# Attention output turned by VectorE in 32x32 blocks straight out of PSUM, put in order by the loads of the next stage, with the join, the expert start and the end re-cut

## The reference

```python
h = rmsnorm(x, g_mix);  z = h @ w_in
o_a = dilated_attention(rope(q_a), rope(k_a), v_a)   # 8 heads of 64
o_b = spatial_gating(uv_b);  o_c = memory_attention(q_c, mem)
o = concat(rmsnorm(o_a), rmsnorm(o_b), rmsnorm(o_c)) * g_out
x = x + o @ w_out
x = x + expert_choice(rmsnorm(x, g_ffn))             # 16 experts, 2*t/16 tokens each
return rmsnorm(x, g_final)
```

## Time and profile before

| | us |
|---|---|
| median of 3 runs | 3288.11 (3286.56 to 3292.55) |
| the profiled execution's own time | 3286.66 |
| its span, first to last instruction | 3284.8 |
| TensorE busy | 3155.9 (96%) |
| VectorE, ScalarE, POOL busy | 1691.6, 1401.4, 731.0 |

### The profile page before, as it was taken

One profiled execution on the slowest core, in us unless ns is written; L12 is line 12 of the kernel. 1 busy time (PEld: TensorE's weight loads), 2 busy tenths in 40 slices (PEclk: granted clock), 3 DMA queues, 4 the chain that ended last, 5 costly groups with the idle time before them and its releaser, 6 DMA issues. The chain is left out here.

```text
span 3284.8 us, 52154 instructions
## 1 busy us (share of the span) xinstructions
PE 3155.9 (96%) x19180; PEld 2749.9 (84%) x19180; DVE 1691.6 (51%) x3631; ACT 1401.4 (43%) x2948; POOL 731.0 (22%) x750
## 2 busy tenths in 40 slices
PE   7999999998999997999689999999999999999996
PEld 5888888886777776888489999999999999999996
DVE  5455545544677775555554444344444344443554
ACT  4333333333788883333343333333333333333443
POOL 0111111113212442222122102222112222112332
PEclk9999999998999998999789999999999999999998
DMA  6222222124744544555347666677666777666895
GB/s 214 61 54 51 55 59 55 47 60 145 242 118 117 161 112 145 189 191 192 118 144 168 142 154 166 165 168 167 136 159 165 168 168 156 144 162 166 230 291 197
DMA packets 389120, 476.13 MB, mean 145 GB/s; under 512 B 131904, under 2 KB 268864, under 8 KB 388800
## 3 DMA queue, kind: packets, MB, share of 16 engines
q1 hardware_dynamic: 368192, 404.35, 45.9%
q0 software_dynamic: 20736, 69.22, 8.4%
HBM read 361.44 MB, written 112.00 MB: 144 GB/s over the span
## 5 line engine op out<-in xcount | busy, mean ns | idle before, releaser
L2115 DVE TENSOR_TENSOR exp_lo<-exp_stage,exp_hi 128x2048 fp32r<-128x2048 f32 x192 | 440.1, 2293 | 566.7 <-ACT exp_hi L1689 566.7
L1689 ACT ACTIVATE exp_hi<-exp_stage 128x2048 fp32r<-128x2048 f32 x192 | 366.6, 1910 | 9.4 <-PE exp_ps_t L2395 4.3
L2380 PE MATMUL exp_ps_g<-exp_xT_hi,exp_lo 128*128 128x384 f32 x1024 | 342.6, 335 | 2.1 <-DVE exp_lo L2115 2.1
L2380 PE MATMUL exp_ps_g<-exp_xT_hi,exp_hi 128*128 128x384 f32 x1024 | 342.3, 334 | 0.0
L2380 PE MATMUL exp_ps_u<-exp_xT_hi,exp_lo 128*128 128x384 f32 x1024 | 342.3, 334 | 0.0
L2380 PE MATMUL exp_ps_g<-exp_xT_lo,exp_hi 128*128 128x384 f32 x1024 | 342.2, 334 | 0.0
L2380 PE MATMUL exp_ps_u<-exp_xT_hi,exp_hi 128*128 128x384 f32 x1024 | 342.1, 334 | 0.0
L2380 PE MATMUL exp_ps_u<-exp_xT_lo,exp_hi 128*128 128x384 f32 x1024 | 342.1, 334 | 0.0
L1926 POOL DMA_INDIRECT scratch_y<-exp_area,route_slots x45 | 91.0, 2023 | 956.4 <-issue 902.0
L1170 ACT ACTIVATE att_prob<-att_prob,att_o 128x256 f32<-128x256 f32 (+1 forms) x576 | 265.8, 464 | 79.2 <-DVE att_o L1212 76.0
L1882 POOL DMA_INDIRECT exp_xe<-scratch_xn,exp_rows_of x180 | 214.8, 1193 | 86.2 <-issue 54.5
(11 more groups left out here) (332 smaller groups left out, 7219.6 us busy)
## 6 DMA issues: line engine op xcount, KB each, us to landing
exp_stage<-in_w_gate SPq DMA_DIRECT2D x256, 256.0 KB, 5.3
exp_stage<-in_w_up SPq DMA_DIRECT2D x256, 256.0 KB, 5.3
exp_stage<-in_w_down SPq DMA_DIRECT2D x256, 256.0 KB, 3.9
out_qT<-scratch_o SPq DMA_DIRECT2D x72, 264.0 KB, 3.0
first_v<-scratch_v SPq DMA_DIRECT2D x64, 256.0 KB, 4.0
scratch_xn<-mix_xn SPq DMA_DIRECT2D x24, 544.0 KB, 3.1
memory_x<-in_x SPq DMA_DIRECT2D x24, 512.0 KB, 3.4
first_v<-scratch_v SPq DMA_DIRECT2D x192, 64.0 KB, 2.2
```

Source lines behind the costliest of these rows:

```text
L1689: self.nc.scalar.activation(self.hi[:, m % self.RW, :, :], self.stage[:, m % self.RS, :, :], ACT.Copy).then_inc(self.hi_sb, 1)
L2115: nc.vector.tensor_tensor(w_lo[:, m % RW, :, :], stage[:, m % RS, :, :], w_hi[:, m % RW, :, :].bitcast(F32), ALU.subtract).then_inc(s["w_l ...
L2380: x_ = nc.tensor.matmul(ps[:, f, 0:S], a[:, m % RW, k, f * P:(f + 1) * P], b[:, k, :], start=(n == 0), stop=(n == 3 * KC - 1))
```

## The change

- `back`, `out_oT` and their buffer go. `out_o` becomes one VectorE transpose in 32x32 blocks, from PSUM to SBUF, waiting for the product itself. Such a transpose moves a block's 32 features onto 32 partitions as queries, and leaves the block's place on the partition axis; so the output's partition axis holds (feature quarter, query), and its columns hold (query quarter, ...). Queries are gathered in a matching order (every fourth one together), the masks, the rows of `w_out` and `g_out` are put into that order ahead of the launch.
- The stores write 512 columns of features and 16 columns of maxima and sums apart, the latter to a new array `stats`: two DMAs a block, and eight for dilation 16 of the sample. For these eight blocks POOL's gather is four copies instead of one.
- The loads of a mixing tile put features in order: 11 DMAs instead of 4. The two that replace `o1` and `o2` are four each (128 pieces of 512 bytes), that of `o0` has 512 pieces.
- The joins of tiles 0 and 1 are spread over the last units of attention (class `Join`), and SP's wait for the last stores moves into mixing, behind its first loads. In every join the last small product is two instructions instead of one, and `scaled3` counts each scaled part.
- Expert start: 8 counting steps ahead of the first product and two in each of units 0 to 3; the turns go tile by tile as each gather lands; the first product waits for five rounds.
- End: the last down product goes tile by tile, and add, square, factor, scale and scatter run as a pipeline over the three tiles. A few semaphores change phase, so that one clearing at the end of the program goes.

```diff
-                    if n % 2 and n > 1:
-                        back(n // 2 - 1)
...
-                    if n % 2 == 0 and n:
-                        out_oT(n // 2 - 1)
...
                 def out_o(c):
-                    dve.wait_ge(back_ps, c + 1)
-                    nc.vector.tensor_copy(o[:, c % RO, 0:D_A], ps_o[:, c % 2, :]).then_inc(o_sb, 1)
+                    dve.wait_ge(pv_ps, 4 * (c + 1))
+                    nc.vector.transpose(o[:, c % RO, 0:D_A], ps_o[:, c % 2, :].rearrange("p (j b i) -> p b j i", j=4, b=QUADS)).then_inc(o_sb, 1)
...
     def load_o(self, sp, A, t, u, seq=0):
...
+        sp.dma_start(to[0], near).then_inc(self.o_loaded[u], 16)
...
+        for a in range(QUADS):
+            sp.dma_start(to[1][:, a, :], mid[a, bass.ds(at * 32, 32)]).then_inc(self.o_loaded[u], 16)
+            sp.dma_start(to[2][:, a, :], far[a, bass.ds(at * 8, 8)]).then_inc(self.o_loaded[u], 16)
+        sp.dma_start(self.o3[:, u, :, D_A:], A["stats"][bass.ds(t * P, P), :, :]).then_inc(self.o_loaded[u], 16)
...
+        T0, T1 = NU - 20, NU - 13
...
+                    for t, at in enumerate((T0, T1)):
+                        if n == at:
+                            join.shift(dve, t, t, 1)
+                        if n == at + 1:
+                            join.divide(dve, t, t)
+                        if at + 2 <= n <= at + 4:
+                            join.scale(dve, t, t, n - at - 2)
+                        if n == at + 6:
+                            join.mean(dve, t)
...
-    FIRST_STEPS = 12
+    FIRST_STEPS = 8
...
+                if m == M - 1 and not more:
+                    for q in range(ST):
...
+                        x_.then_inc(s["tile_done"], 1)
...
+                for q in range(ST):
+                    dve.wait_ge(s["tile_done"], q + 1)
+                    add_end(q, 1)
+                    if q == 0:
+                        mean_end(0)
+                    if q:
+                        scale_end(q - 1)
+                        mean_end(q)
+                scale_end(ST - 1)
```

More of the change, by code:

```diff
@@ L958, in attend_phase @@
+def attend_phase(nc, A, w, early, join, first):
     PIECES = first.PIECES
@@ L1023, in store @@
                     sp.wait_ge(o_sb, c + 1)
-                    for dst, src in blocks[c].outputs(A[f"o{blocks[c].which}"], o[:, c % RO, :]):
+                    for dst, src in blocks[c].outputs(A, o[:, c % RO, :]):
                         sp.dma_start(dst, src).then_inc(o_stored[c % RO], 16)
@@ L1087, in _ @@
                         (lo_w if n % 2 else hi_w)(n // 2)
+                    if c == NB - 4:
+                        nc.gpsimd.memset(join.half[:], -0.5).then_inc(join.s["half_set"], 1)
+                        join.add(pool, 0, 0)
+                    if c == NB - 2:
+                        pool.wait_ge(join.s["half_set"], 1)
+                        join.root(pool, 0)
+                join.add(pool, 1, 1)
+                join.root(pool, 1)
                 pool.wait_ge(w_lo_set, KC)
@@ L1260, in mix_phase @@
         xnT = ph.sb("xnT", [P, KC, P])
[L1261 to L1266, removed]
+        junk, stat, half = join.junk, join.stat, join.half
         ss_y, ms_y, rs_y = stat[:, 100:101], stat[:, 101:102], stat[:, 102:103]
@@ L1350, in fold_lanes @@
                     nc.gpsimd.tensor_tensor(fold[:], fold[:], lane[3], ALU.add).then_inc(s["fold_set"], 1)
[L1352 to L1357, removed]
-                    ge(pool, s["cT_ps"], t - 1)
-                    nc.gpsimd.tensor_tensor(oa[:, u, :], a, c, ALU.add).then_inc(s["added_b"], 1)
-                    pool.wait_ge(s["ms_a"], t + 1)
-                    nc.gpsimd.tensor_tensor(rs_a, ms_a, half[:], ALU.pow).then_inc(s["rs_a"], 1)
                 def norm(t):
@@ L1373, in body @@
                         if not last:
[L1374 to L1376 removed]
+                            join.add(pool, t + 2, u)
+                            join.root(pool, t + 2)
                 fold_lanes()
@@ L1530, in body @@
                         if not last:
-                            join(t + 2, u, i + 2)
+                            join.shift(dve, t + 2, u, i + 2)
+                            join.divide(dve, t + 2, u)
+                            for j in range(3):
+                                join.scale(dve, t + 2, u, j)
                         add_x(t, u, 0, i + 1)
@@ L1864, in _ @@
                 sp.dma_start(g_fin[:], A["g_final"]).then_inc(s["g_loaded"], 16)
-                sp.wait_ge(gathered[0], 16 * ST)
+                for j in range(ST):
+                    sp.wait_ge(first_gathered[j], 16)
                 loop(sp, body)
@@ L1886, in gate @@
                 def gate(e):
-                    pool.wait_ge(gathered[e % 2], gathers(e))
+                    if e:
+                        pool.wait_ge(gathered[e % 2], gathers(e))
+                    else:
+                        for j in range(ST):
+                            pool.wait_ge(first_gathered[j], 16)
                     for a in range(QUADS):
```

380 lines of the change are left out of this document (224 added, 156 removed).

## The result

The changed kernel takes 3343.02 us (median of 4, 3341.63 to 3353.30), against 3288.32 before: ratio 1.0175, 95% interval 1.0155 to 1.0195. It is slower by 55 us where 39 less were forecast. The profiled execution has a span of 3340.3 us.

What follows compares the result with a forecast made beforehand. TensorE bounds attention with dilation 1 and 4 and mixing; a VectorE and ScalarE ring bounds dilation 16. Terms sum to 38.7 us off the profiled 3286.66, 3248.0, so 3249 after allowing for the median; 8 in 10 range 3235 to 3274.

Steps and rivals of the forecast that it cites:

- Attention, TensorE: Dilation 1 and 4 blocks: removing four transposes of `back` saves 0.45 us in each of 48 blocks, 18.0 us after deductions.
- Attention, dilation 16: Dilation 16 blocks: `out_oT` leaves the ring, the transpose takes 0.72 us; 0.43 us a block gained, 10.3 us in all.
- The bound of 1.4 us: Dilation 16: upper bound for the transpose out of PSUM; as a rival (15%), it adds 17 us, giving 3266.
- Attention, costs: Attention: 24 early DMAs instead of 10 lose 2 us (0 to 6); joins of two tiles lose 3 us (0 to 10).
- The hand-over: End of attention to mixing's first product: 9.85 us gained less 1.5 us of SP backlog, 8.3 us (4 to 12).
- The mixing loop: Mixing tiles: SP's 11 loads at 0.43 us, 5.2 us, land before the join needs them; hidden, cost 0.
- the rival on the other side: Mixing: SP's loads become the bound above 1.18 us each; at 1.4 us, 58 us lost, 3307; chance 5%.
- Expert start: Start of experts: first product 0.6 us earlier, four later counting steps cost 1.2; net 0.6 us slower (-1 to +2).
- End: After the last expert product: pipeline over three tiles takes 5.4 us instead of 11.4, 6.0 us gained (4.5 to 7).
- The 0.4 us for the clearing: End of the program: dropping one semaphore clearing gains 0.4 us.

Runs made afterwards that it cites:

- the cut loads of the experiment above: Kernel before, with a tile's dilation 4 and 16 loads cut into four each and dilation 1 into two, 11 DMAs instead of 4, same bytes: 3295.0 us, ratio 1.0026.

## Why the prediction was wrong, step by step

**Attention, TensorE: right for a block.** 6.23 us a block with dilation 1 and 4, 0.44 less. The 18.0 us were too many: the prompt's first 32 blocks brought 11.2, and the sample's first 16, with the early loads spread, 3.4.

**Attention, dilation 16: right for a block, and more.** 4.00 us instead of the 4.14 forecast, and 706 ns for the transpose where 0.72 us was taken. The bound of 1.4 us was not needed.

**Attention, costs: a term mis-sized.** The 24 DMAs were put at 6 us more of SP and 2 us lost; they took 15.6 us of SP where ten took 5, and cost 8. The joins were put at 3 us (0 to 10) and cost about 1. In the changed kernel a VectorE product over 24 columns (L1037) took 2.12 us once, from 1181.27 to 1183.39, while a POOL operation over 1024 columns (L1202) ran from 1180.99 to 1183.36; its median is 0.18. These runs put the whole cost of the joins, such stretching included, at about 1 us.

**The hand-over: a term mis-sized.** Eight stores were priced at 3.6 us and SP's backlog at 1.5 us. Four of the feature stores took 2.7 us and four of the statistics 2.56, so 5.3 a block with the gaps, 6.5 with the values. SP fell behind through all eight blocks and owed 11.8 us at the end. With two stores a block the hand-over was 6.9 us, even better than forecast.

**The mixing loop: the step that failed.** Of the 94 us between the forecast and the result, 64.6 stand here, 19 in attention and 7 in the hand-over. The prediction said "SP's 11 loads at 0.43 ... land near 1415 ... Hidden, 0", and the rival on the other side said that SP decides "once a load costs more than (14 - 1.05) / 11 = 1.18 us". Two things were wrong in that. The price was 0.76 us, not 0.43: the median of 381 ns was that of plain rows, and loads that step through residues were in no row. And the threshold was that of a full queue. SP was never full; the store of `xn` behind the loads closed a ring with VectorE, the turn and the next loads, and in this ring every microsecond past the slack counts at once. The slack can be read from the trace before, had I followed what stands behind the loads on SP. In the tile of the earlier trace rows:

```profile
1408.14 0.33 SPq L945 DMA_DIRECT2D out_qT<-scratch_obc  x1
...
1410.06 0.36 SPq L1308 DMA_DIRECT2D scratch_xn<-mix_xn  x1
...
1415.15 1.28 DVE L1505 SCALAR_TENSOR_TENSOR mix_xn<-out_qT,mix_stat,mix_g_ffn 128x1024 f32<-128x1024 f32 x1 [0.82 <-POOL mix_stat L1366]
```

The store went out 1.6 us after the last load, landed some 3.2 us later (the median) and so was down about 1.9 us before VectorE wrote the buffer again; before the change VectorE never waited for it. That is a slack of some 3.5 us of SP. With 8.4 us of loads from 1406.64 the store could not go before 1415. By this estimate a tile grows by the time of its loads, less the 1.8 us they took before, less 3.5: 0 to 0.2 us for the cut loads of the experiment above (5.3 to 5.5 us; measured 0.3), 3.1 for the 8.4 (measured 3.2 to 4.6 in most tiles, with the slower products in it). The changed kernel has a case between. At the seam of prompt and sample the loads of two tiles stand outside the loop, with no register instructions between them, and take 6.8 us:

```profile
1465.27 0.41 SPq L970 DMA_DIRECT2D out_qT<-scratch_o  x1
...
1471.42 0.60 SPq L977 DMA_DIRECT2D out_qT<-scratch_obc  x1
1472.07 0.43 SPq L1444 DMA_DIRECT2D scratch_xn<-mix_xn  x1
...
1480.59 0.39 SPq L970 DMA_DIRECT2D out_qT<-scratch_o  x1
```

The estimate is 1.5 us more; these tiles take 15.3 and 15.7 us, 1.4 and 1.8 more. And the same loads in another place cost nothing, 332.0 us.

So the rival's mechanism, SP's loads as the bound, was near what happened, at 5%; its price and its point of decision were not. It had asked the right question of the wrong quantity.

**Expert start: small.** Selection gained 2.6 us, not 0.6, and the four late steps cost 1.8, not 1.2 (the first expert takes 103.8 us instead of 102.0). The other 3.8 us of the expert stretch stand in the last expert, 106.6 us instead of 102.7. TensorE waits there for the first weights:

```profile
PE exp_ps_g L2481 <- DVE exp_lo L2204: 4.1, 1, 4.1
```

It was 2.1 us before, 3 to 5 in others, and 6.8 in the kernel before with cut loads, whose last expert took 108.3 us without this change. So it differs from execution to execution; it makes up 2 of the 3.8 us, and the rest is not placed.

**End: right.** Last product to the end of the span 16.2 us instead of 22.0. The 0.4 us for the clearing rested on no row, and no run shows it apart. First add of the last tile and last scatter:

```profile
3324.21 0.75 DVE L2270 SCALAR_TENSOR_TENSOR exp_xe<-exp_ps_t,exp_gates,exp_xe 128x512 f32<-128x512 f32 x1 [0.52 <-PE exp_ps_t L2495]
...
3329.56 0.95 POOL L2029 DMA_INDIRECT out<-exp_xe,route_slots  x1 [0.30 <-issue]
```

6.3 us from the start of the one to the end of the other, where 11.4 stood.

## What to carry to other kernels

Price each DMA issue by a row of the same access pattern, not by the median of the queue (0.56 and 0.64 us a load here, against a median of 0.38), and where there is none take the dearest row as an end that the range must hold. Then ask, before any count of a queue's occupancy, what stands behind the added DMAs in their queue and who waits for its landing: a queue that is idle half of the time can still set the pace when one entry of it closes a ring. Put loads where their data allow, ahead of what is late, and spread a burst over the steps that wait for the same queue.

## What the runs showed of the hardware

SP's time to issue a DMA went with the shape of its access pattern rather than with its pieces or bytes: 0.41 us for 512 pieces of 512 bytes, 0.38 (median of all 240) where eight loads in ten have 128 pieces of 512 or 576 bytes at one stride, 0.56 for 128 pieces in four groups of rows, 0.64 in sixteen, 0.57 for 384 pieces of 64 bytes. Between two of them stood some 0.2 us in the loop and 0.04 outside it. What makes the difference was not taken apart further.

A 32x32-block transpose of 128x512 float32 with its source in PSUM, read in runs of 32 columns out of 128, took 706 ns: the same as from SBUF (708) and 22 ns more than the plain copy (684).

The DMA engines' share in mixing was 0.52 before and 0.48 after, over a stretch a fifth longer, with pieces of the attention parts a quarter as long. With the loads reordered, at the same 181 GB/s as before, it was 0.57: the smaller pieces cost the engines about a tenth more time. No run here shows a loss of the kernel's time from that: with the loads reordered the same small transfers fit into an unstretched tile of 13.87 us.
